# Moving the next head's scores ahead of the step's product in TensorE's order

## What is computed

```python
(a_q, a_k, a_v, a_g, b_q, b_k, b_v, b_g, i_q, i_k, i_w,
 c_q, c_k, c_v, c_g, m_g) = jnp.split(proj, IN_OFFSETS, axis=-1)
s = jnp.einsum('bqhd,bqkd->bqhk', qc, k_g) * scale   # kind B; A and C alike
p = jax.nn.softmax(s_masked, axis=-1)
out = jnp.einsum('bqhk,bqkd->bqhd', p, v_g)
```

## Time and profile before

| | us |
|---|---|
| median of 3 runs | 3378.89 |
| the profiled execution, its own time | 3381.35 |
| span of the profile (first to last instruction) | 3379.6 |
| TensorE busy (matmul) | 3220.0 (95%) |
| VectorE busy | 1769.8 (52%) |
| ScalarE busy | 1168.1 (35%) |
| mean granted TensorE clock | 0.969 of full speed |

### The profile page before, as it was taken

The page is one execution under the profiler, slowest core; times in us unless marked ns, Lnnn a source line. Parts: engine busy times, 40 slices in busy tenths (PEclk is TensorE's granted clock), DMA queues, the critical chain, the costliest instruction groups (busy, mean ns, idle before and its releaser), DMA issues.

```text
span 3379.6 us, 38726 instructions
## 1 busy us (share of the span) xinstructions
PE 3220.0 (95%) x16353; PEld 2662.9 (79%) x16353; DVE 1769.8 (52%) x2488; ACT 1168.1 (35%) x1532; POOL 167.5 (5%) x228
## 2 busy tenths in 40 slices
PE   6999999999999999999999998889989998899899
PEld 5888888798888888887888887656768886567688
DVE  6545543355555543367632346875553458755534
ACT  4222356532223223247421233333442332335322
POOL 0000012200000000012000000000000010000000
PEclk8999999999999999999999998989989999899899
DMA  6555421135554432232222322221212232222132
GB/s 220 185 189 191 133 88 51 38 113 176 194 178 150 162 125 93 88 110 71 92 91 96 100 75 82 80 74 53 67 58 92 81 95 76 69 63 70 56 100 69
DMA packets 287270, 354.23 MB, mean 105 GB/s; under 512 B 9546, under 2 KB 263290, under 8 KB 287098
## 3 DMA queue, kind: packets, MB, share of 16 engines
q1 hardware_dynamic: 287098, 351.75, 32.1%
HBM read 336.52 MB, written 2.10 MB: 100 GB/s over the span
## 4 chain that ended last, share of the span: by engine, by line
PE 84%; DVE 9%; ACT 4%; issue 1%; DMA 1%; POOL 1%; SPq 0%; DVEq 0%; ACTq 0%; POOLq 0%
PE psum L594 56%; PE psum L753 6%; PE psum L711 3%; PE psum L1181 3%; PE psum L635 2%; PE psum L615 2%; PE psum L1048 2%; PE psum L1086 2%; PE psum L851 1%; DVE w_low L1772 1%; PE psum L1064 1%; DVE area L2239 1%; DVE psum L1921 1%; PE psum L560 1%; DVE h_low L1931 1%
## 5 line engine op out<-in xcount | busy, mean ns | idle before, releaser
L594 PE MATMUL psum<-h_high,w_high 128*128 128x512 f32 x2400 | 947.8, 395 | 27.9 <-DVE y_plain L2206 11.6
L594 PE MATMUL psum<-h_low,w_high 128*128 128x512 f32 x2400 | 941.0, 392 | 0.0
L594 PE MATMUL psum<-h_high,w_low 128*128 128x512 f32 x2400 | 940.2, 392 | 0.0
L1772 DVE TENSOR_TENSOR w_low<-raw,w_high 128x2048 fp32r<-128x2048 f32 (+2 forms) x246 | 547.6, 2235 | 301.0 <-ACT w_high L1239 300.8
L1239 ACT CAST w_high<-raw 128x2048 fp32r<-128x2048 f32 (+3 forms) x254 | 464.5, 1841 | 521.5 <-DMA raw<-in_ffn_w_gu 234.6
L594 PEld LDWEIGHTS psum<-h_high,w_high 128*128 128x128 f32 x2400 | 454.1, 189 | 131.9 <-DVE y_plain L2206 12.1
L594 PEld LDWEIGHTS psum<-h_high,w_low 128*128 128x128 f32 x2400 | 453.9, 189 | 97.3
L594 PEld LDWEIGHTS psum<-h_low,w_high 128*128 128x128 f32 x2400 | 454.1, 189 | 94.9 <-issue 1.0
L594 PE MATMUL psum<-y_high,w_high 128*128 128x512 f32 x592 | 232.9, 393 | 7.5 <-DVE y_low L1958 3.6
L2044 DVE TENSOR_TENSOR area<-area,psum 128x512 f32<-128x512 f32 x88 | 60.2, 684 | 340.1 <-PE psum L594 331.7
L594 PE MATMUL psum<-y_high,w_low 128*128 128x512 f32 x592 | 231.4, 391 | 0.0
(11 more groups left out here) (301 smaller groups left out, 4584.4 us busy)
## 6 DMA issues: line engine op xcount, KB each, us to landing
raw<-in_ffn_w_gu SPq DMA_DIRECT2D x88, 1024.0 KB, 5.6
raw<-in_mod_w SPq DMA_DIRECT2D x64, 1024.0 KB, 5.0
raw<-in_w_in SPq DMA_DIRECT2D x64, 1024.0 KB, 5.2
raw<-in_ffn_w_down SPq DMA_DIRECT2D x32, 1024.0 KB, 7.4
raw<-in_ffn_w_down SPq DMA_DIRECT2D x16, 768.0 KB, 4.7
raw<-in_sb_w_qkv SPq DMA_DIRECT2D x12, 1024.0 KB, 5.1
area<-area SPq DMA_DIRECT2D x92, 128.0 KB, 2.3
raw<-in_lru_w_in SPq DMA_DIRECT2D x10, 1024.0 KB, 5.3
```

Source lines behind the costliest of these rows:

```text
L594: mm = e.matmul(psum[0:width, base + m, :], wv[a][:, at_k, c0:c0 + width], X[b][:, k, :], start=(at_k == 0 and (a, b) == (0, 0)), stop=(at ...
L1772: e.tensor_tensor(w_low[raw_at[m]][:, :n], raw[raw_at[m]][:, :n], w_high[x % NW][:, :n].bitcast(F32), ALU.subtract).then_inc(*q.up(s_low, ...
```

## The change

In the loop over steps of both hybrid layers, TensorE's program issues the next head's scores ahead of the step's product. No other engine's program changes, and no wait is added or taken away by name; only the order of two calls is exchanged. In step 23 there is no next head, and in steps without a product the order stays what it was, so 15 steps of each layer change.

```diff
--- before.py
+++ after.py
@@ -1126,9 +1126,9 @@
                     if i >= 2:
                         turns(i - 2)
                     fill_rest(i - 1)
-                    fill(i)
                     if i + 1 < n_heads:
                         scores(i + 1)
+                    fill(i)
                     if i >= 2:
                         values(i - 2)
                 for bank in range(5):
```

## The result

| | before | after |
|---|---|---|
| median, us | 3381.86 (4 runs, 3375.52 to 3392.60) | 3496.05 (4 runs, 3492.42 to 3500.09) |
| profiled execution, us | 3381.35 | 3493.49 |
| span, us | 3379.6 | 3491.8 |
| PE busy, us | 3220.0 | 3277.2 |
| mean granted TensorE clock | 0.969 | 0.953 |

The change makes the kernel slower: the ratio of times is 1.0335, 95% interval 1.0303 to 1.0366. The profiled executions differ by 112.1 us. The direction was forecast, the size was not: 3447 us, with a range up to 3482. One run of the kernel before, beside the last experiment, fell in a slow state (3660.08 us at a granted clock of 0.828) and is left out.

The account below looks back on a forecast made before the run. TensorE, with 84% of the chain, was taken to bound the kernel. 3381.35 + 62.5 us of waits + 6 us of clock gave 3449.9 us for the profiled execution, 3447 us as median; range 3418 to 3482 us.

Parts of the forecast that it names:

- The chain on TensorE, the product as the cover of the wait: Whole kernel: TensorE holds 84% of the chain; in the heads, the 11.1 us product covers the scores' wait for L2287.
- Early scores can't be used early: Heads: L2287 for the next head still needs transposes that stay behind the product; 12 idle times before L2287 show it.
- The price of a step in waits, +62.5 us: Heads: TensorE stalls from the product's new start until L2287 ends; 32.1 us in the first layer, 30.4 in the second.
- The four long steps: Steps 4, 6, 8 and 18: losses of 5.5, 3.4, 4.5 and 5.1 us in the first layer.
- The seven short steps: Steps 9, 12, 13, 15, 16, 20, 21: first-layer stalls of 2.2, 2.5, 1.8, 1.5, 1.1, 1.2, 1.2 us.
- the second half of step 21: Step 21: transposes behind its product hang on its end, so 1.1 us of scores moved ahead aren't given back.
- Step 2: Step 2: product waits 3.15 us for ACT anyway; scores end later than that, loss taken as 0.5 us, between 0 and 1.4.
- Step 5, -2.4 us a layer: Step 5: scores wait 1.9 us and run 2.4 us inside the product's 5.80 us wait, a gain of 2.4 us.
- The clock, +6 us: Heads: slow matmuls behind three stalls of 3.4 to 5.1 us a layer; 3 us a layer taken, bounds 0 and 13.
- The clock rival: Heads: clock falls after every long stall and some short ones, 44 us in place of 6, 3485 us; chance 0.15.
- The rivals on the other side: Heads: early scores are of use, 3330 us, chance 0.03; or product matmuls pass the waiting scores, 3379 us, chance 0.03.
- the first rival: Steps 4, 6, 8, 18: stalls make up for DVE's backlog, 23 us less for both layers, 3424 us; chance 0.14.

Follow-up runs that it names:

- e1: Changed kernel with a first part of the product (1 to 5 of 8 k-tiles, whole in steps 4 and 8) ahead of scores: 3380.77 us, ratio 1.0006.
- e4: Changed kernel, but DVE takes the scores of C heads 13 to 23 early, with L2287 moved ahead in its order: 3453.38 us, ratio 1.0208.
- e5: Kernel before, with scores ahead of the product only in steps 4, 6, 8 and 18 of both layers: 3445.35 us, ratio 1.0179.
- e6: Kernel before, with scores ahead of the product only in steps 9, 12, 13, 15, 16, 20 and 21, both layers: 3426.25 us, ratio 1.0120.
- e2: Changed kernel with throwaway matmuls, 3 to 29 a step, in the stall ahead of the scores: 3455.46 us, ratio 1.0213.
- e3: Kernel before, with scores ahead of the product only in step 5 of both layers: 3377.18 us, ratio 0.9987.
- e9: e6 with throwaway matmuls, 3 to 8 a step, in the stall ahead of the scores: 3407.53 us, ratio 1.0071.

## Why the prediction was wrong, step by step

- **The chain on TensorE, the product as the cover of the wait.** Right. With part of the product as cover the loss is gone (e1), and 109 of 112 us lie in the heads.
- **Early scores can't be used early.** Right. L2287 is released by L1064 12 times, as before, and moving it ahead of those transposes and of DVE's work before it takes the stalls of the C steps away (e4). For the A and B heads it rests on the waits alone.
- **The price of a step in waits, +62.5 us.** Right within its accuracy: PE's time without work grew by 57.6 us. The four long steps were put at 35 us; in the changed kernel their idle times grow by 34.1 us, and e5 shows 34.1 as well. The seven short steps were put at 27 us. Their waits are 21.5 us, in the changed kernel and in e6 alike (the 17.2 of e6 are less because waits of steps 4 and 10, whose order is that of before, shrank by 4.5 us). The predicted stalls ran from the start of the product in the old order, at which the last transposes were still draining, about 0.25 us longer than the idle time that the trace books; that is some 3.5 us of the 6. The rest is the second half of step 21, which isn't a wait of that step. Its first half was right: L2287 of step 21 is 2.06 us late, with the 0.25 the 2.3 that was forecast. The second half, that the 1.1 us of scores are not given back behind the product of step 21, is seen in the first layer of e2, where the clock doesn't blur it: from that product's end to the next one's start 7.08 us pass, as before, though the scores that stood between went ahead. Step 2 was put too low, at 0.5 us a layer: its idle time grew from 3.15 to 5.45 us.
- **Step 5, -2.4 us a layer.** The wait is split as said (e3), and its worth is at the edge of what can be told.
- **The clock, +6 us.** This step failed. It was 51 us. The prediction looked for the clock only behind long stalls: "three stalls of 3.4 to 5.1 us a layer", with the bounds of 0 and 13 us a layer set by these alone, and took 3 of them because one product had kept its clock after 3.15 us of idle time. The runs show that stalls of 0.8 to 2.3 us cost clock as well (e6, e9), and that the fall can come after the stall, in the product, when scores have already run at full speed (step 12 above). Looking whether the first matmuls behind a stall are slow is therefore not enough.

The reading of the rows failed too. The sentence that a stall of 3.4 us or more is followed by slow scores in some steps "and by none in others" gives as others the 3.15 us of step 2, which is not 3.4 or more, and the 5.80 us of step 5, whose product begins with the slow 0.79. Behind all three idle times of 3.4 us or more in the rows (3.44, 4.76 and 5.80 us) TensorE was slow. And that step 2 kept its clock was luck of one layer in one execution. Here is the same product in the second layer of before, the clock in its first 3.3 us (stretch, length, PE busy, clock), and the scores of the step behind it, which take 3.90 us in place of 2.42 after a wait of 1.92 us:

```profile
2860.72 0.50 PE L594 MATMUL psum<-h_high,w_high 128*128 128x512 f32 x1 [3.16 <-ACT area L1633]
2860.70:2864.00 3.30, 3.28 (x9) 0.64 0.00 0
2881.31 3.90 PE L1048 MATMUL psum<-area 64*128 64x128 f32 x8 [1.92 <-DVE area L2287]
```

That product begins with 0.50 us too, and takes 12.79 us instead of 11.20. So the late fall, and the fall behind a short stall, were both in the trace of before. In e5 and e6 the product of step 2 of the first layer, whose order is that of before, takes 13.6 us.

- **The rivals.** The clock rival, 3485 us at a chance of 0.15, was the mechanism that decided beside the waits, but still too small: it counted four short stalls a layer at 2.2 us. The rivals on the other side are out: PE stands at the scores for 7.26 us in step 4 with the product behind them, so no matmuls pass the waiting ones, and the waits for L2287 grew, so the early scores were of no use. DVE's backlog did not shrink by the 23 us of the first rival: the four long steps cost 34.1 us of waits, where 35 were read from the timeline of before.
- **The rule of the Trainium skill** ("TensorE: Matmul & The Clock Gate", Part 1, the clock gate), that the throttled state is the default and activity releases it, fits e2 and e9, where more activity in the same wait kept the clock up: 41 and 17 us back. It was weighed too lightly, against one product that had kept its clock.

## What to carry to other kernels

Before moving work that waits ahead of work that doesn't, read from the timeline what covers the wait now; if the consumer of the early result waits for something behind the moved work anyway, nothing is gained and the whole wait is laid bare. Price each stall of TensorE twice, once for its length and once for the clock: here 57.6 us of idle time brought some 50 us of slower matmuls, and stalls of 1 to 2 us were not exempt. Before taking a step that kept its clock as evidence, look at the same step in the other layer and in other executions: here they differed. If a wait has to stand there, give it a piece of the product as cover.

## What the runs showed of the hardware

Useless matmuls made a kernel faster: 256 of them, in waits that were there anyway, took the time from 3496 to 3455 us. The granted clock fell to 0.50 for 3.2 us after a stall of 2.25 us, not during it (1.00) or right behind it, but in the product 1.8 us later, while scores between had run at 1.00. The same step of the same order can keep its clock or lose it: TensorE is busy for 57.3 us in steps 0 to 3 of the first layer of before, 61.6 us in those of the second, and 63.2 us in those of the first layer of e6. A product of 48 matmuls takes 11.1 to 11.2 us at full clock and 12.8 us with such a start.
